# Final-norm roots of a routed-expert layer: square roots on ScalarE and reciprocals on VectorE, replaced by a power of -0.5 on GpSimd, with one gather made an adding transfer

## What is computed

```python
def rms_norm(x, w):
    y = x * lax.rsqrt(jnp.mean(x * x, axis=-1, keepdims=True) + NORM_EPS)
    return y * w

x = x + pool_mixer(rms_norm(x, norm_mix[0]), pool_w[0], pool_scale[0])
# per token: gate-weighted sum over its 2 experts of (silu(h @ Wg) * (h @ Wu)) @ Wdown
x = x + hier_moe(rms_norm(x, norm_ffn[0]), ...)
return rms_norm(x, norm_final)
```

## Time and profile before

| | |
|---|---|
| median of 3 runs | 683.81 us (683.39 to 685.05) |
| span of the profiled execution | 681.9 us |
| PE busy | 659.4 us (97%) |
| DVE busy | 606.9 us (89%) |
| ACT busy | 527.7 us (77%) |
| POOL busy | 238.3 us (35%) |
| chain that ended last, by engine | PE 88%, DVE 5%, ACT 3%, DMA 2%, issue 2% |
| transfers | 242.62 MB |

### The profile page before, as it was taken

The page is one execution under the profiler, slowest core; times in us unless marked ns, Lnnn a source line. Parts: engine busy times, 40 slices in busy tenths (PEclk is TensorE's granted clock), DMA queues, the critical chain, the costliest instruction groups (busy, mean ns, idle before and its releaser), DMA issues.

```text
span 681.9 us, 10290 instructions
## 1 busy us (share of the span) xinstructions
PE 659.4 (97%) x3638; PEld 556.6 (82%) x3638; DVE 606.9 (89%) x470; ACT 527.7 (77%) x446; POOL 238.3 (35%) x194
## 2 busy tenths in 40 slices
PE   6899989999999999999999999999999999999993
PEld 4899978888888888888888888888888888888872
DVE  6886789899888888889999889988889989898987
ACT  6995527887777778777777788778878888888894
POOL 3000020144444444444444333344333445452401
PEclk9999989999999999999999999999999999999998
DMA  8997869999999999999999999994999999999875
GB/s 296 418 419 254 274 186 421 410 366 377 388 382 382 373 382 378 376 380 380 371 380 389 374 396 382 402 372 158 340 364 380 387 379 378 386 377 389 289 293 202
DMA packets 45155, 242.62 MB, mean 356 GB/s; under 512 B 9719, under 2 KB 10879, under 8 KB 20546
## 3 DMA queue, kind: packets, MB, share of 16 engines
q1 hardware_dynamic: 34322, 220.39, 82.7%
q0 software_dynamic: 10800, 21.80, 11.6%
HBM read 230.34 MB, written 29.36 MB: 381 GB/s over the span
## 4 chain that ended last, share of the span: by engine, by line
PE 88%; DVE 5%; ACT 3%; DMA 2%; issue 2%; POOL 0%; SPq 0%; ACTq 0%; DVEq 0%; POOLq 0%
PE psum L1516 74%; PE psum L1536 4%; PE psum L1444 3%; PE psum L1547 2%; PE psum L1430 2%; PE psum L1462 2%; DMA pw_in<-in_pool_w 1%; DVE raw L1339 1%; PE psum L1453 1%; DMA out<-raw 1%; ACT end_junk L727 1%; DMA xg<-normed,src_all 1%; DVE pw L1037 0%; PE psum L1506 0%; DVE x_rest L999 0%
## 5 line engine op out<-in xcount | busy, mean ns | idle before, releaser
L1083 DVE TENSOR_TENSOR w_lo<-raw,w_hi 128x2048 fp32r<-128x2048 f32 x152 | 345.6, 2291 | 32.6 <-ACT w_hi L795 32.3
L795 ACT ACTIVATE w_hi<-raw 128x2048 fp32r<-128x2048 f32 x152 | 287.9, 1914 | 26.8 <-PE psum L1516 26.8
L1516 PE MATMUL psum<-w_lo,x_hi 128*128 128x512 f32 x616 | 182.8, 392 | 0.0
L651 POOL DMA_INDIRECT total<-ysb,dst_now x29 | 60.6, 2088 | 225.6 <-ACT ysb L875 225.6
L1516 PEld LDWEIGHTS psum<-w_lo,x_hi 128*128 128x128 f32 x616 | 115.1, 188 | 24.9 <-issue 0.5
L1516 PE MATMUL psum<-w_hi,x_hi 128*128 128x512 f32 x408 | 129.5, 399 | 0.0
L1516 PE MATMUL psum<-w_hi,x_lo 128*128 128x512 f32 x408 | 126.1, 390 | 0.0
L1083 DVE TENSOR_TENSOR w_lo<-raw,w_lo 128x2048 fp32r<-128x2048 f32 x40 | 89.9, 2288 | 5.4 <-ACT w_lo L795 5.3
L1516 PE MATMUL psum<-w_lo,h_hi 128*128 128x512 f32 x312 | 92.9, 393 | 0.5 <-DVE h_lo L1288 0.5
L1516 PEld LDWEIGHTS psum<-w_hi,x_lo 128*128 128x128 f32 x408 | 76.6, 188 | 16.8
L1516 PEld LDWEIGHTS psum<-w_hi,x_hi 128*128 128x128 f32 x408 | 72.9, 188 | 16.7 <-DVE w_lo L1083 3.5
(11 more groups left out here) (156 smaller groups left out, 772.5 us busy)
## 6 DMA issues: line engine op xcount, KB each, us to landing
raw<-in_expert_w_gu SPq DMA_DIRECT2D x128, 1024.0 KB, 7.9
raw<-in_expert_w_down SPq DMA_DIRECT2D x64, 1024.0 KB, 7.1
res<-in_x SPq DMA_DIRECT2D x8, 512.0 KB, 9.8
normed<-nx POOLq DMA_DIRECT2D x8, 512.0 KB, 7.5
total<-res SPq DMA_DIRECT2D x8, 512.0 KB, 8.8
raw<-total SPq DMA_DIRECT2D x8, 512.0 KB, 9.2
out<-raw SPq DMA_DIRECT2D x8, 512.0 KB, 3.9
pw_in<-in_pool_w SPq DMA_DIRECT2D x1, 1024.0 KB, 7.7
```

The lines of the kernel that those rows point to most:

```text
L651: pool.indirect_dma_start(out=total[:, :], out_offset=bass.IndirectOffsetOnAxis(ap=dst_now[:].bitcast(u32), axis=0), in_=ysb[:], in_offset ...
L795: nc.scalar.activation(hi_at(s0, j), raw[q][:], ACT.Copy).then_inc(hi_done, 1)
L1083: V.tensor_tensor(w_lo[q][:], raw[q][:], hi_at(s0, j).bitcast(f32), ALU.subtract)\
L1516: last = mm(dst[:, n * N:(n + 1) * N], a[:, ch, :], b[:, c * D + n * N:c * D + (n + 1) * N], start=(ch == 0 and a is hi and b is b_hi), st ...
```

## The change

ACT no longer takes square roots in the final norm and DVE no longer takes reciprocals. ACT only squares, and raises a semaphore `squared`. POOL then makes the mean plus epsilon (a `tensor_scalar` on 128x1) and raises it to -0.5 (a `tensor_tensor` with `pow` against a column of -0.5), and raises `rooted`, for which DVE's norm waits. Eleven roots are thus 22 POOL instructions. ACT's table loads and the one-element silu of the last step go. Four squares instead of three stand ahead of the last silu. The squares write to two scratch tiles in turn.

For step 29's rows POOL no longer gathers into `xg` ahead of the other two. The gathers for steps 30 and 31 come first; then POOL waits until ACT has written `ysb`, and gathers the rows of `total` with an adding transfer onto `ysb`. DVE's addition goes, and the norm of these rows (`late_norm(0)`), with its square on ACT behind silu, moves from the end of DVE's stream to between the fourth tile norm and `h_lo`.

```diff
+        def whole_turn(i, turn):
+            return turn * (TILES + LATE) + i + (1 if i < END_EARLY or turn else 2)
+        def late_turn(k):
+            return TILES + k + 1 if k else END_EARLY + 1
...
             pool.wait_ge(y_stored, 16 * (E - LATE))
-            for k in range(LATE):
+            for k in range(1, LATE):
                 pool.indirect_dma_start(out=late_tile(k), out_offset=None, in_=total[:, :], in_offset=late_rows(k),
...
+            pool.wait_ge(y_copied, E - IN_BANKS)
+            pool.indirect_dma_start(out=ysb[:], out_offset=None, in_=total[:, :], in_offset=late_rows(0),
+                                    bounds_check=TOKENS - 1, oob_is_err=False,
+                                    compute_op=ALU.add).then_inc(late_in[0], 16)
+            def root(turn, sums, means, roots, i):
+                pool.wait_ge(squared, turn)
+                nc.gpsimd.tensor_scalar(means[:, i:i + 1], sums[:, i:i + 1], 1.0 / D, EPS, ALU.mult, ALU.add)\
+                    .then_inc(meant, 1)
+                pool.wait_ge(meant, turn)
+                nc.gpsimd.tensor_tensor(roots[:, i:i + 1], means[:, i:i + 1], minus_half[:], ALU.pow)\
+                    .then_inc(rooted, 1)
+            for i in range(END_EARLY):
+                final_root(i, 0)
+            late_root(0)
+            for i in range(END_EARLY, TILES):
+                final_root(i, 0)
+            for k in range(1, LATE):
+                late_root(k)
             pool.wait_ge(out_stored, 16 * TILES)
...
                         act.wait_ge(pair_used, end_free[TILES // 2])
-                        for i in range(3):
+                        for i in range(END_EARLY):
                             final_square(i, 0)
-                        nc.scalar.activation(warm[:, 1:2], eps[:], ACT.Silu)
...
                     if s0 == E and j == h_split_at(s0):
-                        final_square(3, 0)
+                        late_square_of(0, ysb[:])
                         split_h_block(s - 1, end_free[TILES // 2], hi=h2_hi)
...
             def final_square(i, turn):
                 act.wait_ge(y_in[i], 16 * (turn + 1))
-                root_mean_square(end_junk[:], end_tile(i), i, ss, rs).then_inc(squares3, 1)
+                square_of(whole_turn(i, turn), end_tile(i), i, ss)
...
                     if s0 == E and j == h_split_at(s0):
-                        late_add_copied()
                         final_norm(3, 0)
+                        late_norm(0, ysb[:])
                         low_h(s - 1, hi=h2_hi, lo=h2_lo)
...
             def final_norm(i, turn):
-                dve.wait_ge(squares3, turn * TILES + i + 1)
-                link(V.reciprocal(rs[:, i:i + 1], rs[:, i:i + 1]))
+                dve.wait_ge(rooted, whole_turn(i, turn))
                 V.scalar_tensor_tensor(end_tile(i), end_tile(i), rs[:, i:i + 1], nfin[:],
                                        ALU.mult, ALU.mult).then_inc(out_made, 1)
...
-            for k in range(LATE):
-                late_norm(k)
+            for k in range(1, LATE):
+                late_norm(k, late_tile(k))
```

More of the change, by code:

```diff
@@ L58, in hybrid_pool_moe @@
     LATE, IN_BANKS = 3, 2
+    END_EARLY = 4
     FREE_STEP = E - 10
@@ L134, in hybrid_pool_moe @@
         h2_lo = at("h2_lo", [P, KF, P], f32r, END_H * SLOT + 2 * KB)
-        end_junk = at("end_junk", [P, D], bf16, END_H * SLOT + 4 * KB)
+        end_junk = [at(f"end_junk{n}", [P, D], bf16, END_H * SLOT + (4 + 2 * n) * KB) for n in range(2)]
         XS = 3
@@ L243, in hybrid_pool_moe @@
         root_of_eps = small("root_of_eps", [P, 1], f32)
+        minus_half = small("minus_half", [P, 1], f32)
+        mean = small("mean", [P, TILES], f32)
+        late_mean = small("late_mean", [P, LATE], f32)
         warm = small("warm", [P, 2], f32)
@@ L337, in hybrid_pool_moe @@
         nfin_in = sem("nfin_in")
-        squares3 = sem("squares3")
+        squared = sem("squared")
+        meant = sem("meant")
+        rooted = sem("rooted")
         late_in = [sem(f"late_in{k}") for k in range(LATE)]
         late_sum = sem("late_sum")
-        late_square = sem("late_square")
         late_made = sem("late_made")
@@ L681, in _, with final_root, late_root @@
             pool.wait_ge(y_stored, 16 * (E - LATE))
-            for k in range(LATE):
+            for k in range(1, LATE):
                 pool.indirect_dma_start(out=late_tile(k), out_offset=None, in_=total[:, :], in_offset=late_rows(k),
                                         bounds_check=TOKENS - 1, oob_is_err=False).then_inc(late_in[k], 16)
+            pool.wait_ge(y_copied, E - IN_BANKS)
[9 more added lines that the diff above has]
+                    .then_inc(rooted, 1)
+            def final_root(i, turn):
+                root(whole_turn(i, turn), ss, mean, rs, i)
+            def late_root(k):
+                root(late_turn(k), ss2, late_mean, rs2, k)
+            for i in range(END_EARLY):
[5 more added lines that the diff above has]
+                late_root(k)
             pool.wait_ge(out_stored, 16 * TILES)
@@ L717, in _ @@
                     scatter(v + E, v * 2 + (2 * E - XG - 1), v + E, further=True)
+                for i in range(TILES):
+                    final_root(i, 1)
         @block.scalar
@@ L930, in final_square, with square_of, late_square_of @@
                 act.wait_ge(y_in[i], 16 * (turn + 1))
-                root_mean_square(end_junk[:], end_tile(i), i, ss, rs).then_inc(squares3, 1)
+                square_of(whole_turn(i, turn), end_tile(i), i, ss)
+            def square_of(turn, rows, i, sums):
+                if turn > 2:
+                    act.wait_ge(squared, turn - 2)
+                nc.scalar.activation(end_junk[turn % 2][:], rows, ACT.Square, accum_out=sums[:, i:i + 1])\
+                    .then_inc(squared, 1)
+            def late_square_of(k, rows):
+                if k == 0:
+                    act.wait_ge(late_in[0], 16)
+                else:
+                    act.wait_ge(late_sum, k)
+                square_of(late_turn(k), rows, k, ss2)
             split_next = [FIRST]
@@ L937, in _ @@
             n = act.value_load(n_over[0:1, 0:1], min_val=0, max_val=OVERFLOW)
-            def late_squares(k):
-                act.wait_ge(late_sum, k + 1)
-                root_mean_square(end_junk[:], late_tile(k), k, ss2, rs2).then_inc(late_square, 1)
-            for i in range(4, TILES):
+            for i in range(END_EARLY, TILES):
                 final_square(i, 0)
-            for k in range(LATE):
-                late_squares(k)
+            for k in range(1, LATE):
+                late_square_of(k, late_tile(k))
             with act.If(n):
@@ L1335, in final_norm, with late_norm @@
             def final_norm(i, turn):
-                dve.wait_ge(squares3, turn * TILES + i + 1)
-                link(V.reciprocal(rs[:, i:i + 1], rs[:, i:i + 1]))
+                dve.wait_ge(rooted, whole_turn(i, turn))
                 V.scalar_tensor_tensor(end_tile(i), end_tile(i), rs[:, i:i + 1], nfin[:],
                                        ALU.mult, ALU.mult).then_inc(out_made, 1)
-            def late_add_copied():
-                dve.wait_ge(late_in[0], 16)
-                dve.wait_ge(y_copied, E - IN_BANKS)
-                V.tensor_tensor(late_tile(0), ysb[:], late_tile(0), ALU.add).then_inc(late_sum, 1)
+            def late_norm(k, rows):
+                dve.wait_ge(rooted, late_turn(k))
+                V.scalar_tensor_tensor(late_tile(k), rows, rs2[:, k:k + 1], nfin[:],
+                                       ALU.mult, ALU.mult).then_inc(late_made, 1)
             def late_add(k, y, dn_end):
@@ L1361, in _ @@
             n = dve.value_load(n_over[0:1, 0:1], min_val=0, max_val=OVERFLOW)
-            def late_norm(k):
-                dve.wait_ge(late_square, k + 1)
-                link(V.reciprocal(rs2[:, k:k + 1], rs2[:, k:k + 1]))
-                V.scalar_tensor_tensor(late_tile(k), late_tile(k), rs2[:, k:k + 1], nfin[:],
-                                       ALU.mult, ALU.mult).then_inc(late_made, 1)
             dve.wait_ge(gates_made, 1)
```

6 lines of the change are left out of this document (3 added, 3 removed).

## The result

The changed kernel takes **688.22 us** (median of 4 runs, 687.75 to 689.78), where the kernel before takes 684.38 in the same comparison (4 runs, 683.39 to 685.05). The ratio is 1.0063, with a 95% interval of 1.0051 to 1.0075: slower by 0.6%, where no change was forecast, and 0.8 us above the range's upper end of 687.4. The profiled execution took 688.47 us, with a span of 686.7 against 681.9 before.

The account below looks back on a forecast made before the run. PE bounds the whole run, but the last 30 us hang on a four-engine loop setting the eighth tile norm; ACT's gain is taken by DVE and POOL, summing to 0.0 us: forecast 683.8 us, range 682.0 to 687.4.

Parts of the forecast that it names:

- rival 1: POOL's reads during DVE's norms: not held, or the power slips in; eighth norm 1.6 us earlier, 682.2 us; chance 0.15.
- rival 3: Adding gather onto `ysb`: lands late, costing one for one beyond 660.8 us; landing at 663.5 gives 686.5 us; chance 0.06.
- Rival 4: ACT in the last step: the change doesn't free it, table loads being covered by other waits; no separate chance given.
- Rival 2: POOL's power is slow: 687.4 us at 0.8 us each, threshold 0.58; or a slow first call, about 690; chance 0.19.
- Step 1: Price of one power on POOL, on 128x1: taken as 0.29 us, between bounds of 0.18 and 0.63.
- count of seven: Powers in the chain: three before `hid`, one before step 29's norm, three before the last norms; 0.7 us per 0.1 above 0.29.
- Step 2: Loop of POOL roots and DVE norms: mean slips in behind the root, only the power is held; 1.52 us per norm against 1.39.
- paid in full: Fifth to sixth tile norm: both POOL instructions wait for the fifth norm's end, adding 0.55 us after it.
- Step 3: Behind the eighth tile norm: unchanged, 4.26 us for the store, scatters 1.3 us each, late norms ending near 677.3.
- the 1.1 us that ACT gave back: ACT's last step: without table loads and roots, silu starts about 658.75 instead of 659.86, 1.1 us earlier.

Follow-up runs that it names:

- experiment 4: The changed kernel with the norm weights copied once by ACT into PSUM, so DVE's norms have one SBUF input; 684.53 us, ratio 1.0009 to the kernel before.
- experiment 1: The changed kernel with step 29's rows again gathered early, added on DVE and normed last, roots staying on POOL; 688.9 us, ratio 1.0072 to the kernel before.
- experiment 3: The changed kernel with a multiplication in place of the power on POOL, norms scaled wrongly; 684.63 us, ratio 1.0008 to the kernel before.
- experiment 5: The changed kernel with mean plus epsilon made by ACT, POOL left with the power alone; 685.25 us, ratio 1.0022 to the kernel before.
- experiment 6: The changed kernel with the norm weights in PSUM and the mean made by ACT; 684.0 us, ratio 1.0003 to the kernel before.
- experiment 10: The changed kernel with every power computed twice on POOL, the first result thrown away; 693.1 us, ratio 1.0131 to the kernel before.
- experiment 2: The changed kernel with square roots on ACT and reciprocals on DVE again, its other parts kept; 685.32 us, ratio 1.0015 to the kernel before.
- experiment 8: Against experiment 6: `hid` ahead of the third norm, `h_lo` ahead of step 29's norm, fifth square ahead of `h_hi`; 683.27 us, ratio 0.9990 to the kernel before.
- experiment 9: Against experiment 8: ACT's copy of the norm weights ahead of its wait for PE, step 29's norm behind the late adds; 682.37 us, ratio 0.9980 to the kernel before.

## Why the prediction was wrong

**What held.** ACT is freed, and silu starts as soon as PE is done (0.02 us behind it). `hid` takes over as the late one, and DVE with POOL becomes the loop that sets it. POOL's reads are held by the norms, to 0.04 us after their end; experiment 4 shows the cause, so rival 1 (no hold) is out. The gather was issued 0.7 us later than I had it (650.73, aligned 649.7) and landed 9.1 us after issue, inside the range of the earlier trace rows and 0.4 before its square started; experiment 1 shows that it cost nothing, so rival 3 is out. Rival 4, covered table loads, is out too, as silu did come forward. Rival 2's slow first call is out: the first power took 0.58 us, the others 0.55. The Trainium skill's figure of 6 us for a first call (GPSIMD Engine Reference, Instruction dispatch) is not what this trace shows for this one.

**Step 1, mis-sized: the power's price.** I took 0.29 us between bounds of 0.18 and 0.63; it is 0.55. By the prediction's own count of seven that is 0.26 x 7 = 1.8 us, and 685.6 us: still in the range. The reason I gave for 0.29, an arithmetic instruction on 128x128, was weak: what the instruction computes decides here, 0.55 against 0.19 for a multiplication on the same operands (experiment 3). In the other direction, mean and power are 0.09 apart where I had 0.16.

**Step 2, which failed: "the next mean can slip in right behind the root".** Mostly it can't. After a power both engines are free to go: DVE's norm starts 0.03 us after the power's end (659.31 to 659.34), POOL's next mean 0.08 (to 659.39), and the mean is held. Of the seven intervals from norm to norm up to the eighth tile (leaving out the one across `h_lo`, where the norm waits for a square), four were 2.00, three 1.73 to 1.75. In the prediction one interval paid in full and the others only for the power. That is 0.27 us for each of three more that paid, 0.8 us. Together with step 1 this makes 2.6, where the eighth norm came 2.4 late, aligned; the intervals don't fit one by one, for the one that I had paying in full (fifth to sixth tile) was among the short ones. Experiments 5 and 6 show what the second instruction does: 3.0 us less when the mean leaves POOL, tail included, but only 0.5 where nothing holds it.

**Step 3, which failed: "behind it all is as before".** The prediction noted that the late norms had 1.2 us to spare and then left them alone. But their roots came onto POOL, ahead of the scatters; the last mean is held (1.00 us), and so is the first scatter's issue, probably in reading its index from SBUF. The first scatter is 0.46 us later against the eighth norm than before, and lasts 0.96 longer: 1.4 us, a term that isn't in the sum at all. In experiment 4, without the hold, the first scatter waits for the store again and takes 1.08. The count of seven left out these two roots and those of the fourth and fifth tiles; the traces give eight when the power is made shorter and all eleven when it is made longer (experiments 3 and 10).

**The sum again.** 1.8 + 0.8 + 1.4 = 4.0, against 3.8 aligned in the two profiled spans and 3.8 in the medians of the same comparison (688.22 - 684.38); the forecast of 683.8 is missed by 4.4. The step that put the result outside the range is the third, with the second; my rival 2 had the place right and put its threshold at 0.58 us, which was too high because these two terms were missing from it. The other side of the ledger, the 1.1 us that ACT gave back, went nowhere: silu was early and waited for DVE.

**What stays open.** What sets off the dip of the granted clock near 35 us. It may also be what spreads repeated runs of one kernel: of the kernel before in the comparison of experiments 1 to 4, the seven runs with a mean granted clock of 0.989 took 684.93 to 685.47 us, the 14 with 0.992 or more 683.42 to 684.39. But only profiled executions show their clock by stretch, and experiments 4 and 8, without the dip, still reach the copies of the last step 0.3 and 0.7 us later than the kernel before. What decides that POOL's mean is held beside one norm and not beside another isn't shown either. Which starts first doesn't decide it: the norm of 659.34 started 0.05 ahead of a mean that was held, the norm of 671.16 as much ahead of one that wasn't (671.21, 0.19 us).

## What to carry to other kernels

Before work goes to GpSimd, look at what VectorE does in that moment: if it works through instructions with two SBUF inputs, a GpSimd read mostly waits for the end of one, as here, and a link made of two short GpSimd instructions can be held twice in each turn. One operand in PSUM takes the hold away, if the copy stands where its engine is idle. And when work is appended to an in-order queue, follow it to that queue's last entries: what stood there with slack may now be last.

## What was unexpected of the hardware

- `pow` on GpSimd took 0.55 us on 128x1, a multiplication or scale-and-add 0.19; back to back, a further power adds 0.52. The first power took 0.58.
- A held instruction isn't simply moved: a held mean ended 0.04 us after the norm, a held multiplication 0.05 and a held power 0.42, where they take 0.19, 0.19 and 0.55 alone. By these differences (0.13 to 0.15) a small part of each had been done before the norm let go (an estimate).
- The issue of an indirect transfer on GpSimd is held as well: 1.97 us behind the start of a norm with two SBUF inputs, 1.05 in experiment 9 behind the start of a norm with one, 0.96 to 0.98 with no norm. It ended 0.96 after the norm that was running when it started; a norm that started 0.15 us behind it, in the kernel before, didn't hold it (1.01).
- The granted clock fell to the lower level for some 3.5 us within the first stage in four of 13 profiled executions, with the code there unchanged. In this pair the kernel went from 0.2 us ahead to 1.1 behind across it.
